# A two-layer trunk in fp32: seven-product chunks in two more places of each MLP pass, and down sums taken by ACT and accumulating transfers

## What is computed

```
D_MODEL = 2048
D_FF = 4 * D_MODEL
...
        h = rmsnorm(x, norm_mlp[l])
        x = x + jnp.square(jax.nn.relu(h @ w_up[l])) @ w_down[l]
```

## Time and profile before

| | |
|---|---|
| Median of three runs | 2672.49 us |
| Lowest and highest | 2672.11 and 2678.21 us |
| Profiled execution | 2673.84 us |
| Its span, first to last instruction | 2672.1 us |
| Granted clock of TensorE | 0.999 |
| PE, DVE, ACT busy | 99%, 77%, 54% |
| DMA, mean over the span | 215 GB/s |

### The profile page before, as it was taken

How to read it: one execution, slowest core, us unless ns; L and a number is a source line. 1 busy time by engine, 2 the same in 40 slices (tenths; PEclk the granted TensorE clock), 3 DMA queues, 4 the chain that set the end, 5 groups by cost and what they waited for, 6 DMA issues and landing times.

```text
span 2672.1 us, 37287 instructions
## 1 busy us (share of the span) xinstructions
PE 2657.7 (99%) x13576; PEld 2232.1 (84%) x13576; DVE 2058.7 (77%) x3051; ACT 1445.5 (54%) x1863; POOL 127.6 (5%) x218
## 2 busy tenths in 40 slices
PE   9999999999999999999999999999999999999998
PEld 7788778888888888888888887788888888888887
DVE  5676568977898897987756755689678988989875
ACT  5545555545565555645445455555456556556554
POOL 0100000000100100100010000000001001000000
PEclk9999999999999999999999999999999999999999
DMA  7885545676775766766687655466677767667574
GB/s 259 235 238 169 178 162 187 225 238 236 236 232 194 238 219 208 240 205 236 227 234 227 219 175 172 161 200 225 228 252 234 229 205 239 209 218 233 190 248 152
DMA packets 179961, 575.56 MB, mean 215 GB/s; under 512 B 23016, under 2 KB 43028, under 8 KB 179664
## 3 DMA queue, kind: packets, MB, share of 16 engines
q1 hardware_dynamic: 166256, 536.94, 61.3%
q0 software_dynamic: 13008, 35.98, 5.1%
q10 hardware_dynamic: 528, 0.37, 0.1%
HBM read 535.15 MB, written 38.04 MB: 215 GB/s over the span
## 4 chain that ended last, share of the span: by engine, by line
PE 92%; DVE 4%; DMA 2%; ACT 1%; issue 1%; SPq 0%; POOLq 0%; POOL 0%; ACTq 0%
PE acc L527 24%; PE acc L529 23%; PE acc L528 23%; PE att L495 2%; PE att L497 2%; PE att L496 2%; PE acc L495 2%; PE acc L497 2%; PE acc L496 2%; PE acc L544 1%; PE acc L543 1%; PE acc L545 1%; DVE w_lo L1311 1%; DMA raw<-in_w_main 1%; DVE w_lo L1332 1%; PE turn L496 1%
## 5 line engine op out<-in xcount | busy, mean ns | idle before, releaser
L1311 DVE TENSOR_TENSOR w_lo<-raw,w_hi 128x1024 fp32r<-128x1024 f32 (+1 forms) x778 | 934.8, 1212 | 410.9 <-ACT w_hi L886 409.0
L886 ACT ACTIVATE w_hi<-raw 128x1024 fp32r<-128x1024 f32 (+1 forms) x778 | 813.4, 1051 | 655.8 <-PE acc L529 485.9
L527 PE MATMUL acc<-w_hi,h_hl 128*128 128x512 f32 x1848 | 736.2, 398 | 0.4 <-DVE w_lo L1311 0.3
L529 PE MATMUL acc<-w_hi,h_hl 128*128 128x512 f32 x1848 | 729.0, 394 | 0.0
L528 PE MATMUL acc<-w_lo,h_hl 128*128 128x512 f32 x1848 | 728.5, 394 | 0.0
L527 PEld LDWEIGHTS acc<-w_hi,h_hl 128*128 128x128 f32 x1848 | 347.9, 188 | 82.7 <-issue 4.6
L529 PEld LDWEIGHTS acc<-w_hi,h_hl 128*128 128x128 f32 x1848 | 347.9, 188 | 81.3
L528 PEld LDWEIGHTS acc<-w_lo,h_hl 128*128 128x128 f32 x1848 | 348.3, 188 | 76.0
L1332 DVE TENSOR_TENSOR w_lo<-raw,w_hi 128x1792 fp32r<-128x1792 f32 x166 | 335.5, 2021 | 38.7 <-ACT w_hi L895 37.8
L527 PE MATMUL acc<-w_hi,o_hl 128*128 128x512 f32 x912 | 360.9, 396 | 0.0
L528 PE MATMUL acc<-w_lo,o_hl 128*128 128x512 f32 x912 | 359.9, 395 | 0.0
(11 more groups left out here) (298 smaller groups left out, 3504.7 us busy)
## 6 DMA issues: line engine op xcount, KB each, us to landing
raw<-in_w_main SPq DMA_DIRECT2D x928, 512.0 KB, 4.2
scratch<-spread SPq DMA_DIRECT2D x37, 512.0 KB, 2.7
moved<-scratch SPq DMA_DIRECT2D x148, 128.0 KB, 3.2
scratch<-spread POOLq DMA_DIRECT2D x30, 512.0 KB, 3.6
moved<-scratch POOLq DMA_DIRECT2D x120, 128.0 KB, 4.9
raw<-in_w_misc SPq DMA_DIRECT2D x16, 336.0 KB, 4.4
bias_b<-bias_rows POOLq DMA_DIRECT2D x32, 96.0 KB, 5.7
xs<-in_x SPq DMA_DIRECT2D x4, 512.0 KB, 7.2
```

The costliest lines, as they stand in the source:

```text
L527: nc.tensor.matmul(o, a_hi, hi[:, kk], start=(k == 0), stop=False)
L529: last = nc.tensor.matmul(o, a_lo, hi[:, kk], start=False, stop=fin)
L886: nc.scalar.activation(w_hi[s][:, 0:2 * width], raw[r][:, 0:2 * width], ACT.Copy).then_inc(hi_ready, 1)
L1311: nc.vector.tensor_tensor(w_lo[s][:, 0:2 * width], raw[r][:, 0:2 * width], w_hi[s][:, 0:2 * width].bitcast(F32), ALU.subtract).then_inc(lo ...
```

## The change

Four edits come together. First, the tables of seven-product chunks: the first up unit of a pass goes from three to four, the second from none to two, the first down unit from two to three, so 24 chunks more over both layers. The second up unit now uses the side banks `wide_acc[1]`, the third `wide_acc[0]`. Second, what followed the second up unit moves: its result is now summed (`add_up_sides`) in the next pass, and `u_moved` of the first up unit moves from the third up unit's third chunk to the end of the second up unit. Third, `take_down` moves from DVE to ACT: ACT copies both side banks to `stage` and both main banks to `down_main` (the memory of `spread`), and POOL adds them to `rest` and to x by two accumulating transfers, `add_down`. ACT waits for the transfers of the take before. Fourth, PSUM banks are allocated in pairs, and operations on two halves become one of 1024 values; the loops of SP, ACT and DVE are written out.

```diff
-WIDE_UP = ((1, 3, 5), (), (1, 3, 5, 7), ())
-WIDE = ((1, 3), (1, 3, 5, 7), (1, 3, 5, 7), (1, 3, 5, 7))
+WIDE_UP = ((1, 3, 5, 7), (1, 3), (1, 3, 5, 7), ())
+SIDES_OF_UP = (0, 1, 0)
+WIDE = ((1, 3, 5), (1, 3, 5, 7), (1, 3, 5, 7), (1, 3, 5, 7))
 AT_UP2, AT_UP0, AT_DOWN = 0, len(WIDE_UP[2]), len(WIDE_UP[2]) + len(WIDE_UP[0])
 WIDE_AT = tuple(AT_DOWN + sum(len(w) for w in WIDE[:n]) for n in range(NBLK))
-N_WIDE = AT_DOWN + sum(len(w) for w in WIDE)
+AT_UP1 = AT_DOWN + sum(len(w) for w in WIDE)
+N_WIDE = AT_UP1 + len(WIDE_UP[1])
...
-            return ctx.enter_context(nc.psum_tensor(name, [P, NB], F32))
+            return ctx.enter_context(nc.psum_tensor(name, [P, TT * NB], F32))[:].rearrange("p (t c) -> p t c", t=TT)
...
+        down_main = spread[:].rearrange("p j k t s -> p (j k t s)").rearrange("p (t c) -> p t c", t=TT)
...
-        acc = [[psum(f"acc{s}{t}") for t in range(TT)] for s in range(2)]
-        turn = psum("turn")
-        att = [psum(f"att{i}") for i in range(3)]
-        wide_acc = [(att[0], att[1]), (att[2], turn)]
+        acc_pair = [psum(f"acc{s}") for s in range(2)]
+        acc = [[pair[:, t, :] for t in range(TT)] for pair in acc_pair]
+        wide_pair = [psum("att01"), psum("att2_turn")]
+        wide_acc = [[pair[:, t, :] for t in range(TT)] for pair in wide_pair]
+        att, turn = [*wide_acc[0], wide_acc[1][0]], wide_acc[1][1]
...
-                with sp.Fori(0, GROUPS - 1) as g:
+                for g in range(GROUPS - 1):
...
+            def add_down(l, g, n):
+
+                pool.wait_ge(down_out, downs_before(l, g, n) + 1)
+                pool.dma_start(rest[:, n], stage[:], accum_op=ALU.add).then_inc(down_added, 16)
+                pool.dma_start(xs[:, :, n * NB:(n + 1) * NB], down_main, accum_op=ALU.add).then_inc(down_added, 16)
...
-                for n in range(POOL_MOVES):
+                pass_on(l, E_U)
+                for g in range(GROUPS - 1):
+                    for n in range(NBLK):
+                        pass_on(l, E_U + g * NBLK + n + 1)
+                    for n in range(NBLK):
+                        add_down(l, g, n)
+                for n in range((GROUPS - 1) * NBLK + 1, POOL_MOVES):
...
+                def downs(g, n):
+                    return lambda: pe.wait_ge(down_out, downs_before(l, g, n) + 1)
...
-                         sides=wide_acc[n // 2])
+                         sides=wide_acc[SIDES_OF_UP[n]] if wide else None)
...
-                    down(g * 64 + (C_MLP + 56), 1, adds(g, 1), 2, wide=WIDE[2])
-                    down(g * 64 + (C_MLP + 64), 0, adds(g, 2), 3, wide=WIDE[3])
-                    up(g * 64 + (C_MLP + 72), 1, adds(g, 3), 1)
+                    down(g * 64 + (C_MLP + 56), 1, downs(g, 0), 2, wide=WIDE[2])
+                    down(g * 64 + (C_MLP + 64), 0, downs(g, 1), 3, wide=WIDE[3])
+                    up(g * 64 + (C_MLP + 72), 1, downs(g, 2), 1, wide=WIDE_UP[1])
...
+                    if n == 1:
+                        act.wait_ge(down_added, downs_before(l, g, 0) * 32)
...
+                def take_down(g, n, end):
+
+                    unit_done(end)
+                    if n == 0:
+                        act.wait_ge(spread_ready, l * MOVES + E_U + (g + 1) * NBLK + 1)
+                        act.wait_ge(pool_stored, (l * POOL_MOVES + (g + 1) * NBLK + 1) * 16)
+                    else:
+                        act.wait_ge(down_added, downs_before(l, g, n) * 32)
+                    nc.scalar.activation(stage[:], wide_pair[1 - n % 2], ACT.Copy)
+                    nc.scalar.activation(down_main, acc_pair[1 - n % 2], ACT.Copy).then_inc(down_out, 1)
...
+                    else:
+                        run(g * 64 + (C_MLP + 16), {3: lambda: take_side(g, 1, end + 16), 6: lambda: take_summed(g, 1, sides_count(g, -1))},
+                            {0: lambda: u_sums_hi(g, 0)}, WIDE_UP[2], steps_at(g, AT_UP2))
...
-                    for n in range(1, NBLK):
-                        run(g * 64 + (C_MLP + 40 + 8 * n), wide=WIDE[n], steps=steps_at(g, WIDE_AT[n]))
-                    run(g * 64 + (C_MLP + 72))
+                    run(g * 64 + (C_MLP + 48), (), {3: lambda: take_down(g, 0, end + 48)}, WIDE[1], steps_at(g, WIDE_AT[1]))
+                    run(g * 64 + (C_MLP + 56), {7: lambda: take_down(g, 1, end + 56)}, (), WIDE[2], steps_at(g, WIDE_AT[2]))
+                    run(g * 64 + (C_MLP + 64), (), {7: lambda: take_down(g, 2, end + 64)}, WIDE[3], steps_at(g, WIDE_AT[3]))
+                    run(g * 64 + (C_MLP + 72), (), {5: lambda: take_down(g, 3, end + 72), 7: lambda: u_moved(g, 4)},
+                        WIDE_UP[1], steps_at(g, AT_UP1))
                 g, end = GROUPS - 1, base + 64 * (GROUPS - 1)
-                run(C_MLP + 64 * g + 16, {3: lambda: take_up(g, 1, end + 16, 1)}, {2: lambda: u_moved(g, 0)},
-                    WIDE_UP[2], steps_at(g, AT_UP2))
-                run(C_MLP + 64 * g + 24, {3: lambda: take_side(g, 2, end + 24), 4: lambda: take_summed(g, 2, sides_count(g, 0))},
-                    {2: lambda: u_moved(g, 1)})
+                run(C_MLP + 64 * g + 16, {3: lambda: take_side(g, 1, end + 16), 5: lambda: take_summed(g, 1, sides_count(g, -1))},
...
-                for t in range(TT):
-                    last = nc.vector.transpose(spread[:, :, :, t, :].rearrange("p j k s -> p k j s"),
-                                               src[:, t, :].rearrange("p (k j s) -> p k j s", k=PIECES, j=QUARTERS))
-                last.then_inc(spread_ready, 1)
+                nc.vector.transpose(spread[:].rearrange("p j k t s -> p t k j s"),
+                                    src.rearrange("p t (k j s) -> p t k j s", k=PIECES, j=QUARTERS)).then_inc(spread_ready, 1)
...
+                    bank = acc_pair[n % 2]
...
-                    nc.vector.tensor_tensor(stage[:, 0, :], acc[0][0][:], stage[:, 0, :], ALU.add)
                     dve.wait_ge(up_step, steps + 3)
-                    nc.vector.tensor_tensor(stage[:, 1, :], acc[0][1][:], stage[:, 1, :], ALU.add).then_inc(up_summed, 1)
+                    nc.vector.tensor_tensor(stage[:], bank, stage[:], ALU.add).then_inc(up_summed, 1)
...
-                def take_sides(n):
-
-                    for t in range(TT):
-                        nc.vector.tensor_tensor(rest[:, n, t, :], wide_acc[1 - n % 2][t][:], rest[:, n, t, :], ALU.add)
...
-                def take_down(g, n, end):
-                    dve.wait_ge(multiplied, end + SLOTS)
-                    take_sides(n)
-                    add_to_x(end, n, bank=1 - n % 2)
...
+                    else:
+                        run(g * 64 + (C_MLP + 16), (),
+                            {1: lambda: u_sums_lo(g, 0), 3: lambda: add_up_sides(g, 1, NBLK - 1), 6: lambda: spread_u(g, 1)},
+                            WIDE_UP[2], steps_at(g, AT_UP2))
...
-                    run(g * 64 + (C_MLP + 48), (), {3: lambda: take_down(g, 0, end + 48)}, WIDE[1], steps_at(g, WIDE_AT[1]))
-                    run(g * 64 + (C_MLP + 56), {7: lambda: take_down(g, 1, end + 56)}, (), WIDE[2], steps_at(g, WIDE_AT[2]))
-                    run(g * 64 + (C_MLP + 64), (), {7: lambda: take_down(g, 2, end + 64)}, WIDE[3], steps_at(g, WIDE_AT[3]))
-                    run(g * 64 + (C_MLP + 72), (), {5: lambda: take_down(g, 3, end + 72)})
+                    run(g * 64 + (C_MLP + 48), (), (), WIDE[1], steps_at(g, WIDE_AT[1]))
+                    run(g * 64 + (C_MLP + 56), (), (), WIDE[2], steps_at(g, WIDE_AT[2]))
+                    run(g * 64 + (C_MLP + 64), (), (), WIDE[3], steps_at(g, WIDE_AT[3]))
+                    run(g * 64 + (C_MLP + 72), (), {7: lambda: u_moved(g, 4, g < GROUPS - 2)},
+                        WIDE_UP[1], steps_at(g, AT_UP1))
                 g = GROUPS - 1
-                run(C_MLP + 64 * g + 16, (), {2: lambda: u_moved(g, 0, False), 3: lambda: spread_u(g, 1)},
+                run(C_MLP + 64 * g + 16, (), {3: lambda: add_up_sides(g, 1, NBLK - 1), 5: lambda: spread_u(g, 1)},
```

93 lines of the change are left out of this document (53 added, 40 removed).

## The result

The changed kernel takes 2713.34 us (median of four runs, 2712.26 to 2715.75), the kernel before beside it 2674.25 us: ratio 1.0146, 95% interval 1.0133 to 1.0158. The prediction of 2677 with a range of 2667 to 2692 missed.

The account below looks back on a forecast made before the run. TensorE was taken as the bound, busy 99% of the span. Products -7.0, first down stalls +7.2, last group +2.0 and transfers +2 sum to +4.2 on 2673.84 us: 2678.0, less 1.35 to the median, 2677 us; range 2667 to 2692.

Parts of the forecast that it names:

- The products, -7.0: TensorE, MLP units: four more seven-product chunks a pass save 1.17 us, over six passes -7.0 us.
- The stall of 1.2 us a pass in the first down unit, +7.2: First down unit: DVE's subtractions end late, TensorE stalls 1.04 us at the fourth chunk, 0.16 more at the next.
- 1 us of cover for a load in the first down unit: First down unit's second weight sums: they start 5.2 us after their slot came free, against a load's 4.2 us.
- The relief is in the down units, the load in the first up and first down unit: DVE's work: total nearly even, but its places shift; each added seven-product chunk costs DVE 2.34 us.
- the 2.0 forecast: Last group's third up unit: 12.8 us of work against TensorE's 7.8 and lead 4.0; stall 1.0, twice, +2.0 us.
- Transfers, +2: POOL's accumulating pairs: 10 us a pair, hitting weight loads by a third of a microsecond a pass, +2 us.
- the 16 given as the upper end: Transfer pair's time to landing: at most three plain 512 KB stores in a row for each pair, some 16 us.
- nobody waits: Takes on ACT: at 10 us a pair no wait, since the shortest gap, third to fourth take, leaves 10.2 us.
- ACT's takes at nothing: Takes moved to ACT: two copies of about 1.25 us each, costed at nothing, with ACT's 9 idle us as cover.
- Accumulating transfers hold ACT: Slower rival: ACT's fourth take waits for the third's transfers; at 16 us a pair, 36 more, 2713 us; chance 0.18.
- Weights land late: Slower rival: shared DMA engines make weight loads take 6 to 8 us, not 4.2; 2683 to 2689 us; chance 0.20.
- DVE keeps up: Rival: DVE's chain has 1.5 us of unseen slack, so stalls vanish; 2665.5 us; chance 0.12.

Follow-up runs that it names:

- e7: Kernel before with only two added seven-product chunks, the first up unit's fourth and the first down unit's third: 2692.21 us, ratio 1.0065.
- e2: Changed kernel with the takes back on DVE as two additions of 1024 values, no accumulating transfers, all 24 added chunks kept: 2692.52 us, ratio 1.0063.
- e3_no_transfers: Changed kernel with ACT's copies kept but a tiny memset in place of each take's two accumulating transfers: 2693.05 us, ratio 1.0062.
- e6_second_up_only: Kernel of e2 with the first up unit's fourth and first down unit's third seven-product chunk taken back, the second up unit's two kept: 2681.43 us, ratio 1.0022.
- e16: Kernel of e2 with three seven-product chunks in first up, second up and first down units, two in third up; one last-group transpose earlier: 2672.32 us, ratio 0.9988.
- e14: Kernel of e2 with seven-product chunks moved: three in the first up unit, four in the second, three in the third: 2692.15 us, ratio 1.0054.
- e5_plain: Changed kernel with each take's two accumulating transfers made plain copies of the same bytes: 2693.18 us, ratio 1.0061.
- e12_long_rows: Changed kernel with the second accumulating transfer going to another block of rest, rows of 4096 B, instead of x, rows of 2048 B: 2697.96 us, ratio 1.0084.
- e8_third_left_out: Changed kernel with the third take's two transfers of each pass replaced by two of 4 bytes: 2701.57 us, ratio 1.0096.

## Why the prediction was wrong

- **The products, -7.0.** Right. First-pass units run at 21.04, 22.30 and 21.06 as forecast, and the 39.9 us of the spans are 46.9 of stalls less these 7.0.
- **The stall of 1.2 us a pass in the first down unit, +7.2.** Right for the two tables alone (8.1 in e7), 10.1 in the full change. The failed step is that the walk of DVE's queue ended there. It made TensorE late by 1.2 us and left DVE with no lead, and TensorE stalls again at or just behind the second down unit: 7.3 us in e7, 6.2 in the change. With takes on DVE (e7, e2) it is the take, nine chunks further on, that stands where the lead was 1.46. In the change the take is ACT's, and the stall comes behind DVE's waits for weight loads: 1.89 us at that chunk in the second pass, 2.35 to 2.94 us ahead of the third down unit's start in four others. The prediction had 1 us of cover for a load in the first down unit and priced nothing behind it. For the take the rows were there; the walk had to go on until the lead was back at four slots.
- **"The relief is in the down units, the load in the first up and first down unit".** The second failed step. The second up unit's side sums, 2.7 us, were priced for the last group alone, where the 2.0 forecast came out (2.7 in e3_no_transfers). They stand in the third up unit of every later pass too, and there they take the lead with which the first up unit was assumed to begin (1.04 to 1.15 us, 3.3 to 3.7 before). A wait for a weight load takes more of it, the last seven-product chunk starts without any, and first up units of later passes stall 8.1 us, where the forecast had none. In e6_second_up_only, with such waits but three chunks in this unit, it is 0.7.
- **Transfers, +2.** The pair's 10 us were about right (the second lands in 10.3 us from its own issue, some 11 from the first's), though the working was not: three stores of 3.6 us in a row are 10.8, not the 16 given as the upper end. The conclusion "nobody waits" was wrong: it took the issue for granted. POOL issued the second transfer of the third take 5.8 to 7.5 us late, 10 became 16, over the 10.2 us of the gap. Cost: 20, not 2.
- **ACT's takes at nothing** held in the sum (1.0 us a copy, not 1.25; e2 and e3 are equal in time). The merged instructions and written-out loops were not run alone, but e16 has both and stalls 1.3 us in all.
- **Rivals.** "Accumulating transfers hold ACT" gave 2713 at 16 us. Both numbers were met, and that is luck: the rival's 36 us are 20 here, of which at most some 12 go by its mechanism, DVE's queue makes the other 17, and its 16 us come from a late issue that it does not name. A rival whose number is hit still needs the run that takes its cause away. "Weights land late" happened as well (59.3 us of DVE's waits, against 24.7 in e3_no_transfers), though a load lands in 4.3 us in the median, not in 6 to 8. "DVE keeps up" fell in every pass.

Open: why POOL's issue waits at the third take of each pass, why single weight loads come late where DVE has lost its lead, and how the transfers' 20 us divide exactly between ACT's wait, short rows and late weights. A version with separate buffers for the third and fourth take was not tried.

## What to carry to other kernels

Walk an in-order queue to the point where its lead is back at the bound that its buffers set, not to the first stall: two edits that cost 4 and 0 us alone cost 17 together because both drew on the same lead. On that walk, look at the waits for loads too: the changed kernel lost a part of its lead at them. Put extra work where the lead is at its bound, and take the same amount away where it is thin; e16 got its chunks that way. Moving alone is not enough: e14 moved its 25 chunks and gained nothing. Price a transfer that someone waits for from the data being ready to the landing, issue included, and an accumulating one at over twice the engine time of a plain one.

## What was not expected of the hardware

- Accumulating and plain transfers of the same 19920 packets in the POOL queue: 10.0% and 7.2% of the engines' span, landing 6.7 and 9.0 us against 5.5 and 6.4; 25 MB of plain copies, beside the weights at 225 GB/s in all (e5_plain, 300 to 2600 us), cost no time.
- A wait for "issue" of 5.8 to 7.5 us at the same transfer of each pass, unmoved by twice the descriptor memory, though that removed five of seven such waits elsewhere. With other rows at the destination (e12_long_rows) it stood before two transfers of each pass, and without the third pair (e8_third_left_out) before none but one of 1.0 us.
- 48 POOL additions, 136 us of POOL, made DVE 87 us busier (2153.9 against 2066.4 in e3_no_transfers) at the same instructions.
